# Splitting the value products of the prompt attention into fp32r halves, and moving the softmax weighing to GpSimd

## The chip, the cores and the metric

The kernel runs on one core of a Trainium2 chip. The metric is the device time of one execution in microseconds (us); lower is better. A core has five engines that run their own instruction lists and meet only through semaphores: TensorE (PE, matrix products and transposes, results in PSUM), VectorE (DVE), ScalarE (ACT), GpSimd (POOL) and SyncE (SP, here only DMA issue). PSUM has 8 banks of 128 partitions by 512 fp32 numbers; in this kernel `psA` to `psD` are two banks each, and `bank[0]` to `bank[7]` counts through them.

## The reference

One step of a one-layer decoder trunk in fp32, for a prompt of 1024 tokens and for 8 x 4 sampled tokens that share the weights. The input projection feeds a convolution group, a pooling group and an attention group ("NSA") of 8 query heads in 2 key/value groups of 4 heads, head size 64. The attention of the prompt has three branches, each with its own keys and values:

```python
s = jnp.einsum('bqgrd,bngd->bgrqn', q, kc).astype(jnp.float32) * scale + tbl[:, :, t5_bucket(dist)]
p_cmp = masked_softmax(s, dist >= 0)                       # compressed blocks, 63 keys
o_cmp = jnp.einsum('bgrqn,bngd->bqgrd', p_cmp.astype(vc.dtype), vc)
...                                                        # selected blocks: all earlier keys here
p = masked_softmax(s, (dist >= 0)[:, :, None])
o_slc = jnp.einsum('bgrqm,bgqmd->bqgrd', p.astype(vg.dtype), vg)
...                                                        # window of 512 keys
p = masked_softmax(s, mask)
o_win = jnp.einsum('bgrqk,bkgd->bqgrd', p.astype(vw.dtype), vw)
return gates[:, :, 0] * o_cmp + gates[:, :, 1] * o_slc + gates[:, :, 2] * o_win
```

Behind it come the output projection, RMSNorm, a gated feed-forward network of width 2816 and a last RMSNorm. With 1024 tokens there are 16 blocks of 64 keys, and the top-k takes 16, so the selected branch attends to every earlier key.

## The kernel before

The program is written out by hand for each engine; nothing is scheduled by a tool. It goes through stages: transposes and the input projection (to about 245 us), the sampled tokens (to about 345 us), the attention of the prompt (345 to 617 us), the output projection (to about 725 us), the feed-forward network and the last norm. The change is in the prompt attention and at its edges.

The prompt has 8 query tiles of 128 tokens (`i` = 0 to 7). For each, `ORDER` lists five groups: (g=0, br=1), (g=0, br=2), compressed, (g=1, br=1), (g=1, br=2). Branch 1 sees `128*(i+1)` keys, branch 2 at most 640. The compressed group serves both g at once. The four others are "dense": 32 dense groups, called by their number q in `DENSE`. `steps()` makes four steps for each q, one for each head r. In a step PE computes the scores of head (q, r) and then works off "tiles" of the group three places earlier (`LAG = 3`): a tile is 128 keys of all four heads, and the tiles of a group are spread over its four steps. There are 132 dense tiles and 8 compressed ones.

What happens to one head: PE writes the scores into PSUM (`p_score`, L1017 and L1018, two fp32r products), DVE adds the bias and finds the maximum (`p_biased_max`, L1814 to L1820), ACT takes the exponential into SBUF (`p_exp`, L1415, one step later), DVE computes 1/sum times the gate for a whole group (`group_weights`, L1858 and L1861) and multiplies each head by it (`weigh_head`, L1867). What happens to one tile: PE transposes 128 x 128 of each of the four heads into one turn bank (`turn`, L731), ACT copies the bank to one of three SBUF buffers `probT` (`drain`, L1312), and PE multiplies it with 128 columns of `kvtok`, two tiles later in its list (`p_values`, L1037 in plain fp32; L1028 for the compressed tile). The values of g=0 stand in columns 0 to 63 and those of g=1 in columns 64 to 127, with zeros beside them, so that one bank (6) collects both groups. `turn_bank` gives the tiles banks 4, 5 and 7 in turn, `turn_free` says which earlier tile must have been drained. When a query tile is complete ACT copies bank 6 to `featT` (`out_tile`, L1421) and PE may start the next.

fp32r is a format in which a product takes one pass over the array and loses low bits. Elsewhere in this kernel exactness is kept by splitting a number into a high part, which is its fp32r rounding, and a low part, the rest.

GpSimd's only work ahead of this stage is at L2127 to L2151: it places the values in `kvtok` (four instructions), splits keys and queries into high and low parts, and is then idle until the scores are done. SP waits for the split keys before it distributes them (`load_keys`, L649). At the end of the stage DVE makes the low parts of the first two output weight tiles (`rest_w`, L1884) and then those of the features (L1909), for which `fH` (L1457) comes from ACT.

## Time and profile before

| | |
|---|---|
| median of 3 runs | 1512.11 us (1511.27 to 1513.88) |
| profiled execution | 1512.36 us |
| its span, first to last instruction | 1510.2 us |
| busy: PE, DVE, ACT, POOL | 1451.0, 759.1, 477.7, 219.2 us |
| granted TensorE clock, mean | 0.987 |

The profiled execution is 2.2 us longer than its span, which is what lies around the program. "Busy" counts the time in which at least one instruction of the engine is recorded; neighbouring instructions of one engine overlap a little in the records, so the distance between two starts is the better measure of what one costs. A matrix product in plain fp32 is recorded as two instructions. Clock 1.00 is the granted TensorE clock at its upper level, 0.50 at the lower.

### The profile page before, as it was taken

How to read it: one execution, taken by the hardware profiler on the slowest of the kernel's cores; microseconds unless marked ns; L12 is line 12 of the kernel's file. 1: busy time of each engine (PE TensorE's matmuls, PEld its weight loads, DVE VectorE, ACT ScalarE, POOL GpSimd, SP SyncE). 2: the span in 40 equal slices, each digit the busy share in tenths (PEclk: the TensorE clock that was granted, in tenths of full speed). 3: DMA queues.
4: the chain of work that ended last, by engine and by line, in shares of the span. 5: the costliest groups of instructions: out<-in, count | busy, mean ns of one | idle time of the engine just before them, and what ended most of it. 6: DMA issues, size and time to landing. Idle time of an engine off the chain costs nothing.

```text
span 1510.2 us, 22117 instructions
## 1 busy us (share of the span) xinstructions
PE 1451.0 (96%) x8743; PEld 1330.9 (88%) x8743; DVE 759.1 (50%) x1535; ACT 477.7 (32%) x961; POOL 219.2 (15%) x251
## 2 busy tenths in 40 slices
PE   6999999888999999899999999999999999999996
PEld 6999988656666666699999999999999999999996
DVE  5499933226887776322424443524253344435257
ACT  5122124236776666422311211211121112111123
POOL 2114102520000000044220101010100101010105
PEclk9999999999999999999999999999999999999998
DMA  8731114943111102232110211202020202112012
GB/s 204 192 78 30 45 31 125 303 112 77 43 28 29 29 1 43 55 87 74 54 46 22 63 39 50 63 26 73 11 74 19 70 22 64 42 46 67 18 49 115
DMA packets 165815, 98.98 MB, mean 66 GB/s; under 512 B 35650, under 2 KB 160537, under 8 KB 165633
## 3 DMA queue, kind: packets, MB, share of 16 engines
q1 hardware_dynamic: 163217, 88.71, 21.5%
q0 software_dynamic: 2496, 8.88, 2.2%
q8 instruction: 69, 1.13, 0.3%
q14 instruction: 33, 0.27, 0.1%
HBM read 78.33 MB, written 13.19 MB: 61 GB/s over the span
## 4 chain that ended last, share of the span: by engine, by line
PE 82%; DVE 7%; SPq 3%; DMA 3%; ACT 2%; issue 2%; POOL 0%; POOLq 0%; DVEq 0%; ACTq 0%
PE psA L1065 16%; PE psB L1065 16%; PE psC L1065 16%; PE psD L1037 6%; PE psC L731 4%; DVE ybuf L1653 4%; DMA zraw<-in_w_in 2%; PE psD L731 2%; PE psA L782 2%; PE psA L1094 2%; PE psB L1094 2%; PE psC L1094 2%; PE psB L782 2%; PE psC L782 2%; PE psB L1017 1%
## 5 line engine op out<-in xcount | busy, mean ns | idle before, releaser
L1429 ACT CAST wH<-wraw 128x1024 fp32r<-128x1024 f32 (+1 forms) x132 | 86.7, 658 | 262.2 <-PE psC L1065 176.4
L2174 POOL TENSOR_TENSOR hid<-hid,rstdB 128x352 f32<-128x352 f32 x66 | 74.8, 1162 | 629.1 <-ACT hid L1490 629.1
L1037 PE MATMUL psD<-probTb,kvtok 128*128 128x512 f32 x264 | 135.7, 597 | 2.2 <-ACT featT L1421 2.1
L1884 DVE TENSOR_TENSOR wL<-wraw,wH 128x1024 fp32r<-128x1024 f32 (+1 forms) x132 | 107.2, 813 | 44.7 <-ACT wH L1429 44.7
L1065 PE MATMUL psA<-gH,wH 128*128 128x352 f32 x352 | 113.7, 323 | 0.0
L1065 PE MATMUL psB<-gH,wH 128*128 128x352 f32 x352 | 113.7, 323 | 0.0
L1065 PE MATMUL psC<-gH,wH 128*128 128x352 f32 x352 | 113.5, 322 | 0.0
L1065 PE MATMUL psA<-gH,wL 128*128 128x352 f32 x352 | 113.2, 322 | 0.0
L1065 PE MATMUL psB<-gH,wL 128*128 128x352 f32 x352 | 113.1, 321 | 0.0
L1065 PE MATMUL psA<-gL,wH 128*128 128x352 f32 x352 | 113.1, 321 | 0.0
L1065 PE MATMUL psB<-gL,wH 128*128 128x352 f32 x352 | 112.9, 321 | 0.0
L1065 PE MATMUL psC<-gL,wH 128*128 128x352 f32 x352 | 112.8, 321 | 0.0
L1065 PE MATMUL psC<-gH,wL 128*128 128x352 f32 x352 | 112.8, 320 | 0.0
L1653 DVE SCALAR_TENSOR_TENSOR ybuf<-glu,convw,ybuf 128x1296 f32<-128x1296 f32 x60 | 103.3, 1766 | 0.7
L1939 DVE TENSOR_TENSOR hid<-psA,rstdB 128x352 f32<-128x352 f32 x44 | 21.0, 520 | 160.7 <-PE psB L1065 160.6
L1947 DVE TENSOR_TENSOR hid<-psB,hid 128x352 f32<-128x352 f32 x22 | 11.5, 525 | 167.4 <-PE psC L1065 167.4
L1490 ACT ACTIVATE hid<-hid 128x352 f32<-128x352 f32 x66 | 29.9, 499 | 204.9 <-DVE hid L1939 204.9
L1312 ACT COPY probTb<-psC 128x512 f32<-128x512 f32 (+2 forms) x104 | 58.8, 565 | 46.7 <-PE psC L731 46.4
L1494 ACT CAST aH<-hid 128x352 fp32r<-128x352 f32 x66 | 31.5, 487 | 122.8 <-DVE hid L1947 121.8
L1065 PEld LDWEIGHTS psA<-gL,wH 128*128 128x128 f32 x352 | 66.4, 189 | 0.0
L1065 PEld LDWEIGHTS psB<-gH,wL 128*128 128x128 f32 x352 | 66.2, 188 | 0.0
L1065 PEld LDWEIGHTS psA<-gH,wH 128*128 128x128 f32 x352 | 66.0, 188 | 0.2
(426 smaller groups left out, 3898.7 us busy)
## 6 DMA issues: line engine op xcount, KB each, us to landing
wraw<-in_w_gu SPq DMA_DIRECT2D x44, 512.0 KB
wraw<-in_w_down SPq DMA_DIRECT2D x80, 128.0 KB
zraw<-in_w_in SPq DMA_DIRECT2D x12, 512.0 KB
xa<-in_x_prompt SPq DMA_DIRECT2D x8, 512.0 KB, 8.4
pages<-in_cache_cmp_kv SPq DMA_DIRECT2D x32, 128.0 KB, 2.4
qS<-qH SPq DMA_DIRECT2D x32, 128.0 KB, 2.4
qS<-qL SPq DMA_DIRECT2D x32, 128.0 KB, 2.4
xs<-in_x_prompt SPq DMA_DIRECT2D x8, 512.0 KB, 3.8
```

Source lines behind the costliest of these rows:

```text
L731: return pe.transpose(dst, src, ident[0:n, 0:n])
L782: mm = pe.matmul(bank[3 * (m % 2) + n][:, 0:w], wt[:, m % 2, k, :], mv[:, k, c0:c0 + w], start=(k == 0 and wt is zH and mv is xH), stop=(k ...
L1037: mm = pe.matmul(o, kvtok[:, kt, vc:vc + P], pt, start=first, stop=((g, br) == ORDER[-1] and x == len(g_tiles(n)) - 1))
L1065: mm = pe.matmul(bank[3 * par + n][:, 0:cw], wt[:, par, k, :], mv[:, k, at:at + cw], start=(k == 0 and mv is mH and wt is wH), stop=(k == ...
L1094: mm = pe.matmul(b[:, 0:cw], wt[:, par, k, :], mv[:, k, c0:c0 + cw], start=False, stop=(k == KD - 1 and wt is wL))
L1312: op = sc_.copy(dst, srcfn(bank[turn_bank(u)]))
L1429: sc_.copy(wH[:, par, 0:nk, :], wraw[:, par, 0:nk, :]).then_inc(s["wH_done"], 1)
L1490: sc_.activation(hid[:, n, :], hid[:, n, :], ACT.Silu).then_inc(s["silu_done"], 1)
L1494: sc_.copy(aH[:, par, x // 2, at:at + cw], hid[:, n, :]).then_inc(s["aH_done"], 1)
L1653: op = dve.scalar_tensor_tensor(out=y, in0=x, scalar=w, in1=y, op0=ALU.mult, op1=ALU.add)
L1884: dve.tensor_tensor(wL[:, par, 0:nk, :], wraw[:, par, 0:nk, :], wH[:, par, 0:nk, :].bitcast(F32), ALU.subtract).then_inc(s["wL_done"], 1)
L2174: pool.tensor_tensor(hid[:, n, :], hid[:, n, :], rstdB[:, c0:c0 + cw], ALU.mult).then_inc(s["up_scaled"], 1)
```

## The change

Values: GpSimd writes each value block as 64 high and 64 low columns into `vS` (which lies over `kvtok`) with 64 small instructions that wait for one another. Each group g now has an accumulator bank of its own, 6 and 7. The tile is kept as `probH`, ACT's fp32r rounding of the turn bank, and `probL`, which a new DVE instruction per tile (`rest_tile`) computes as bank minus `probH`. A value product becomes two fp32r products of 128 x 512. The result stands in two halves of the bank (with high values and with low values), which ACT (`out_half`) and DVE (`out_sum`) add into `featT`, for each (i, g).

The compressed product becomes two fp32 products, on rows 0 to 63 and 64 to 127, into the two banks. The turn banks are 4 and 5 only; a dense turn bank is free when `rest_tile` has read it. The weighing of 112 of 128 heads goes to GpSimd, which does them group after group; head 3 of the 16 dense groups of query tiles 0 to 3 stays on DVE.

```diff
@@ -245,7 +251,7 @@
 
     if U_C <= u < U_C + 2 * NB:
         return 4 + (u - U_C) % 4
-    return 4 + u % 2 if u < U_T else (4, 5, 7)[(u - U_T) % 3]
+    return 4 + u % 2
 
 
 def turn_free(u):
...
@@ -254,10 +260,13 @@
         return u - 4 if u >= U_C + 4 else U_C - 1
     if U_C + 2 * NB <= u < U_C + 2 * NB + 2:
         return U_C + 2 * NB - 1
-    return u - 2 if u < U_T else U_T - 1 if u < U_T + 3 else u - 3
-
-
-OUT_AFTER = {i: max(u for k, u in PUNIT.items() if k[0] == "t" and GROUPS[k[1]][0] == i) for i in range(NT)}
+    return u - 2
+
+
+OUT_AFTER = {(i, g): max(u for k, u in PUNIT.items() if k[0] == "t" and GROUPS[k[1]][:2] == (i, g))
+             for i in range(NT) for g in range(KVH)}
+BY_DVE = [(n, GQ - 1) for n in DG if GROUPS[n][0] < 4]
+DENSE_T = {k: m for m, k in enumerate([k for k in PUNIT if k[0] == "t" and k[1] in DENSE])}
 
 
 LASTQ = [(n, m) for n in range(3) for m in range(KD)]
...
@@ -369,6 +378,9 @@
         vcT = at("vcT", [P, KC_N - 1], 166144)
         vctok = at("vctok", [P, 3, P], 167424)
         probT = [probTb[:, k, :] for k in range(NPT)]
+        probH = at("probH", [P, NPT, 512], 158720, F32R)
+        probL = [at(f"probL{k}", [P, 512], o, F32R) for k, o in enumerate((54528, 164864, M_S + 2528))]
+        vS = at("vS", [P, NT + 1, KVG], M_Z, F32R)
         cmpw = at("cmpw", [P, 3, 8, P], 168960)
         cmph = at("cmph", [P, 2, KC_N], 158720)
         cmps = at("cmps", [P, 2, KC_N], 161312)
...
@@ -472,7 +484,9 @@
 
         def wait_drained(eng, key):
 
-            if key in DRAINED_D:
+            if key in DENSE_T:
+                eng.wait_ge(s["pl_done"], DENSE_T[key] + 1)
+            elif key in DRAINED_D:
                 eng.wait_ge(s["turn_drain_d"], DRAINED_D[key])
             else:
                 eng.wait_ge(s["turn_drain"], DRAINED_A[key])
...
@@ -1021,21 +1035,25 @@
             def p_values(n, x):
 
                 i, g, br = GROUPS[n]
-                pt = probT[PUNIT[("t", n, x)] % NPT]
+                slot = PUNIT[("t", n, x)] % NPT
                 wait_drained(pe, ("t", n, x))
-                o = bank[6]
                 if br == 0:
-                    mm = pe.matmul(o, vcBD, pt, start=False, stop=False)
+                    if i:
+                        pe.wait_ge(s["o_ev"], 2 * i)
+                    pt = probT[slot]
+                    pe.matmul(bank[6], vcBD[0:HD, :], pt[0:HD, :], start=False, stop=False)
+                    mm = pe.matmul(bank[7], vcBD[HD:P, :], pt[HD:P, :], start=True, stop=False)
                 else:
                     first = x == 0 and (g, br) == ORDER[0]
                     if first and i == 0:
-                        pe.wait_ge(s["v_pad"], 4)
+                        pe.wait_ge(s["v_pad"], 4 * 2 * NT)
                     elif first:
-                        pe.wait_ge(s["o_ev"], i)
+                        pe.wait_ge(s["o_ev"], 2 * i - 1)
                     kt = x if br == 1 else i + 1 - g_width(n) // P + x
                     vc = 256 * br + P * g
-                    mm = pe.matmul(o, kvtok[:, kt, vc:vc + P], pt, start=first,
-                                   stop=((g, br) == ORDER[-1] and x == len(g_tiles(n)) - 1))
+                    last = br == 2 and x == len(g_tiles(n)) - 1
+                    pe.matmul(bank[6 + g], vS[:, kt, vc:vc + P], probH[:, slot, :], start=first, stop=False)
+                    mm = pe.matmul(bank[6 + g], vS[:, kt, vc:vc + P], probL[slot][:, :], start=False, stop=last)
                 mm.then_inc(s["probT_used"], 1)
 
             for _, _, jobs, tiles in steps():
...
@@ -1044,7 +1062,8 @@
                 for n, x in tiles:
                     if n in DENSE:
                         if x == 0:
-                            pe.wait_ge(s["scaled"], GQ * (DENSE[n] + 1))
+                            pe.wait_ge(s["scaled"], weighed(DENSE[n])[0])
+                            pe.wait_ge(s["scaled_d"], weighed(DENSE[n])[1])
                         turn(("t", n, x), [(P * r, P, prob(n, r)[:, P * x:P * x + P]) for r in range(GQ)])
                     else:
                         pe.wait_ge(s["cmp_scaled"], GROUPS[n][0] + 1)
...
@@ -1415,11 +1434,12 @@
                 sc_.activation(prob(n, r)[:, 0:w], p_scores(n, r)[:, 0:w], ACT.Exp,
                                bias=nmax[:, job % 4:job % 4 + 1], scale=-1.0, accum_out=psums[q % 4][:, r:r + 1]).then_inc(s["exp_done"], 1)
 
-            def out_tile(i):
-
-                sc_.wait_ge(s["probT_used"], OUT_AFTER[i] + 1)
-                sc_.copy(featT[:, 4:8, P * i:P * i + P], bank[6].rearrange("p (r t) -> p r t", r=GQ)
-                         ).then_inc(s["o_ev"], 1)
+            def out_half(i, g):
+
+                sc_.wait_ge(s["probT_used"], OUT_AFTER[i, g] + 1)
+                gp, other = slice(HD * g, HD * g + HD), slice(HD * (1 - g), HD * (1 - g) + HD)
+                sc_.copy(featT[gp, 4:8, P * i:P * i + P], bank[6 + g][other, :].rearrange("p (r t) -> p r t", r=GQ)
+                         ).then_inc(s["o_half"], 1)
 
             def round_w(w, par, nk):
...
@@ -1854,7 +1874,8 @@
                 rc = precs[q % 4]
                 dve.wait_ge(s["exp_done"], NSJ + LASTJOB[n] + 1)
                 if q >= 4:
-                    dve.wait_ge(s["scaled"], GQ * (q - 3))
+                    dve.wait_ge(s["scaled"], weighed(q - 4)[0])
+                    dve.wait_ge(s["scaled_d"], weighed(q - 4)[1])
                 dve.reciprocal(rc, psums[q % 4]).then_inc(s["sum_read"], 1)
                 dve.wait_ge(s["sum_read"], q + 1)
                 c = KVC + NH * br + GQ * g
@@ -1864,14 +1885,22 @@
             def weigh_head(n, r):
 
                 p = prob(n, r)[:, 0:g_width(n)]
-                dve.tensor_scalar(p, p, precs[DENSE[n] % 4][:, r:r + 1], None, ALU.mult).then_inc(s["scaled"], 1)
-
-            def turn_copy(key):
-
-                pu = PUNIT[key]
-                dve.wait_ge(s["turn_fill"], UNIT[key] + 1)
-                dve.wait_ge(s["probT_used"], pu - NPT + 1)
-                dve.tensor_copy(probT[pu % NPT], bank[4 + UNIT[key] % 2]).then_inc(s["turn_drain_d"], 1)
+                dve.tensor_scalar(p, p, precs[DENSE[n] % 4][:, r:r + 1], None, ALU.mult).then_inc(s["scaled_d"], 1)
+
+            def rest_tile(n, x):
+
+                key = ("t", n, x)
+                slot = PUNIT[key] % NPT
+                dve.wait_ge(s["turn_drain"], DRAINED_A[key])
+                dve.tensor_tensor(probL[slot][:, :], bank[turn_bank(UNIT[key])], probH[:, slot, :].bitcast(F32), ALU.subtract
+                                  ).then_inc(s["pl_done"], 1)
+
+            def out_sum(i, g):
+
+                gp = slice(HD * g, HD * g + HD)
+                o = featT[gp, 4:8, P * i:P * i + P]
+                dve.wait_ge(s["o_half"], 2 * i + g + 1)
+                dve.tensor_tensor(o, bank[6 + g][gp, :].rearrange("p (r t) -> p r t", r=GQ), o, ALU.add).then_inc(s["o_ev"], 1)
 
             def link2(op):
                 chain[0] += 1
@@ -1894,12 +1923,17 @@
                 if 0 <= old < len(DG):
                     if head == 0:
                         group_weights(DG[old])
-                    weigh_head(DG[old], head)
+                    if (DG[old], head) in BY_DVE:
+                        weigh_head(DG[old], head)
                 if r == 3 and rider(q) is not None:
                     c_scale(rider(q))
                 for n, x in tiles:
-                    if ("t", n, x) in DRAINED_D:
-                        turn_copy(("t", n, x))
+                    if n in DENSE:
+                        rest_tile(n, x)
+                    for o, last in OUT_AFTER.items():
+                        if last == PUNIT["t", n, x] - 4:
+                            out_sum(*o)
+            out_sum(NT - 1, 1)
             for w in range(2):
                 rest_w(w, w, KD)
...
@@ -2122,13 +2156,6 @@
 
             pool.wait_ge(s["qbd_done"], 1)
             pool.wait_ge(s["stores"], 16 * STORES)
-            for br in (1, 2):
-                c = 256 * br
-                pool.tensor_copy(kvtok[:, 0:NT, c:c + HD], kvtok[:, 0:NT, c + P:c + P + HD]).then_inc(s["v_pad"], 1)
-            for br in (1, 2):
-                c = 256 * br
-                pool.wait_ge(s["v_pad"], br)
-                pool.memset(kvtok[:, 0:NT, c + HD:c + HD + P], 0.0).then_inc(s["v_pad"], 1)
             pool.wait_ge(s["cmpw_used"], 4)
             pool.memset(pcmp, 0.0).then_inc(s["prob_zero"], 1)
...
@@ -2138,6 +2165,23 @@
                 count[0] += 1
                 op.then_inc(s["pool"], 1)
                 pool.wait_ge(s["pool"], count[0])
+
+            pads = [0]
+
+            def pad(op):
+
+                pads[0] += 1
+                op.then_inc(s["v_pad"], 1)
+                pool.wait_ge(s["v_pad"], pads[0])
+
+            for i in range(NT):
+                for br in (1, 2):
+                    c = 256 * br
+                    for g in range(KVH):
+                        v = kvtok[:, i, c + P + HD * g:c + P + HD * g + HD]
+                        vh = vS[:, i, c + P * g:c + P * g + HD]
+                        pad(pool.tensor_copy(vh, v))
+                        pad(pool.tensor_tensor(vS[:, i, c + P * g + HD:c + P * g + P], v, vh.bitcast(F32), ALU.subtract))
 
             old = slice(0, T)
             in_turn(pool.tensor_copy(keysH[:, :, :], keysT[:, :, old]))
...
@@ -2149,9 +2193,16 @@
                 cols = slice(P * i, P * i + P)
                 pool.tensor_tensor(qL[:, :, cols], qT[:, :, cols], qH[:, :, cols].bitcast(F32), ALU.subtract
                                    ).then_inc(s["split_done"], 1)
+            for q, n in enumerate(DG):
+                pool.wait_ge(s["rec_done"], q + 1)
+                for r in range(GQ):
+                    if (n, r) in BY_DVE:
+                        continue
+                    p = prob(n, r)[:, 0:g_width(n)]
+                    pool.tensor_scalar(p, p, precs[q % 4][:, r:r + 1], None, ALU.mult).then_inc(s["scaled"], 1)
             pool.wait_ge(s["score_mm"], NSJ + NJ)
             pool.memset(xs[0][:, NT, :], 0.0).then_inc(s["x_pad"], 1)
-            pool.wait_ge(s["o_ev"], NT)
+            pool.wait_ge(s["o_ev"], 2 * NT)
```

Three places show how the instructions stand in each engine's list. First VectorE, in the steps behind the compressed weighing of query tile 5 (`psA`, `psB` are score banks, `ISA` is the bias and minimum in one instruction, `narrow` and `wide` hold exponentials). Before:

```order
TENSOR_TENSOR narrow<-narrow,small_115 128x8x47
TENSOR_REDUCE small_115<-psA 128x1
ISA psA,nmax<-psA,btab,small_115 128x256
ISA nmax 128x1
TENSOR_SCALAR wide<-wide,small_115 128x768
TENSOR_REDUCE small_115<-psB 128x1
ISA psB,nmax<-psB,btab,small_115 128x256
ISA nmax 128x1
RECIPROCAL small_115<-small_115 128x4
TENSOR_TENSOR small_115<-small_115,kvtok 128x4
TENSOR_SCALAR narrow<-narrow,small_115 128x640
```

Now, at the same place:

```order
TENSOR_TENSOR narrow<-narrow,small_120 128x8x47
TENSOR_TENSOR probL_105<-psC,probH 128x512
TENSOR_REDUCE small_120<-psA 128x1
ISA psA,nmax<-psA,btab,small_120 128x256
ISA nmax 128x1
TENSOR_TENSOR probL_106<-psC,probH 128x512
TENSOR_TENSOR probL_107<-psC,probH 128x512
TENSOR_REDUCE small_120<-psB 128x1
ISA psB,nmax<-psB,btab,small_120 128x256
ISA nmax 128x1
RECIPROCAL small_120<-small_120 128x4
```

The weighing (`TENSOR_SCALAR`) is gone from the list, and one subtraction from a turn bank stands there for each tile of the step.

Second TensorE, in the last query tile. `cpk` is the identity, so rows with it are the transposes of a tile; `kS` marks scores. Before:

```order
MATMUL psC<-cpk,narrow 128x128 x4
MATMUL psD<-probTb,kvtok 128x512
MATMUL psC<-cpk,narrow 128x128 x4
MATMUL psD<-probTb,kvtok 128x512
MATMUL psB<-kS,qS_111 128x512
```

Now:

```order
MATMUL psC<-cpk,narrow 128x128 x4
MATMUL psD<-probH,vS 128x512
MATMUL psD<-probL_107,vS 128x512
MATMUL psC<-cpk,narrow 128x128 x4
MATMUL psD<-probH,vS 128x512
MATMUL psD<-probL_105,vS 128x512
MATMUL psB<-kS,qS_116 128x512
```

One product per tile has become two, and the place of the scores between them is the same.

Third VectorE at the end of the stage, where `wL` are the output weights' low parts and `fL` those of the features. Before:

```order
TENSOR_SCALAR wide<-wide,small_115 128x1024 x2
RECIPROCAL small_115<-small_115 128x4
TENSOR_TENSOR small_115<-small_115,kvtok 128x4
TENSOR_SCALAR narrow<-narrow,small_115 128x640 x4
TENSOR_TENSOR wL<-wraw,wH 128x1024 x2
TENSOR_TENSOR fL<-featT,fH 128x1056 x8
```

Now:

```order
TENSOR_TENSOR probL_105<-psC,probH 128x512
TENSOR_TENSOR probL_106<-psC,probH 128x512
TENSOR_TENSOR probL_107<-psC,probH 128x512
TENSOR_TENSOR featT<-psD,featT 64x4x128
TENSOR_TENSOR wL<-wraw,wH 128x1024 x2
TENSOR_TENSOR fL<-featT,fH 128x1056 x8
```

The two `wL` instructions now stand behind the last tile's work and the last sum of halves.

## Rows read from the trace of the kernel before

**Rows 1.** Busy time by stretches of the stage (us from:to, length, engines, clock).

```profile
345.00:371.50 26.50, 23.03 (x125) 18.20 (x123) 21.17 (x122) 18.79 (x73) 0.00 (x0) 0.87 0.24 61
371.50:581.20 209.70, 202.97 (x1005) 141.14 (x1005) 167.57 (x496) 144.58 (x309) 0.00 (x0) 1.00 0.11 26
581.20:617.00 35.80, 35.68 (x166) 21.38 (x163) 11.70 (x26) 19.75 (x37) 0.21 (x1) 1.00 0.23 45
```

**Rows 2.** The same view of L1867 alone, VectorE's weighing.

```profile
371.50:581.20 209.70, 49.49 (x94) 1.00 0.11 26
```

**Rows 3.** TensorE in order of time (start, length): fp32r scores, transposes, value product.

```profile
567.55 0.40 PE L1017 MATMUL psA<-kS,qS 128*128 128x512 f32 x1
...
568.02 0.60 PE L731 MATMUL psC<-cpk,narrow 128*128 128x128 f32 x4
568.46 1.02 PE L1037 MATMUL psD<-probTb,kvtok 128*128 128x512 f32 x2
569.32 0.60 PE L731 MATMUL psC<-cpk,narrow 128*128 128x128 f32 x4
```

**Rows 4.** VectorE in order of time in the first stage: a bank minus its rounding.

```profile
25.16 1.27 DVE L1614 TENSOR_TENSOR xL<-psD,xH 128x512 fp32r<-128x512 f32 x2
26.36 1.26 DVE L1605 SCALAR_TENSOR_TENSOR xn<-xa,small,gB 128x1024 f32<-128x1024 f32 x1
```

**Rows 5.** VectorE in order of time: finding the least, and weighing.

```profile
541.20 0.56 DVE L1818 TENSOR_REDUCE small<-psA 128x1 f32<-128x384 f32 x1
541.80 0.49 DVE L1820 CUSTOM_DVE_ANT_0 psA<-psA,btab,small 128x256 f32<-128x256 f32 x1
...
549.75 0.55 DVE L1867 TENSOR_SCALAR narrow<-narrow,small 128x640 f32<-128x640 f32 x1
550.22 0.95 DVE L1818 TENSOR_REDUCE small<-psB 128x1 f32<-128x768 f32 x1
```

**Rows 6.** Order of time behind the last scores: casts, a turn, its drain.

```profile
597.68 2.00 ACT L1429 CAST wH<-wraw 128x1024 fp32r<-128x1024 f32 x2
...
601.70 0.60 PE L731 MATMUL psC<-cpk,wide 128*128 128x128 f32 x4
...
602.39 0.58 ACT L1312 COPY probTb<-psC 128x512 f32<-128x512 f32 x1 [0.71 <-PE psC L731]
```

**Rows 7.** Order of time at the end of the stage.

```profile
616.39 0.49 PE L1088 MATMUL psA<-cpk,xs 128*128 128x128 f32 x3
...
616.59 0.59 ACT L1421 COPY featT<-psD 128x512 f32<-128x512 f32 x1 [1.94 <-PE psD L1037]
...
618.18 2.43 DVE L1909 TENSOR_TENSOR fL<-featT,fH 128x1056 fp32r<-128x1056 f32 x2 [17.05 <-ACT fH L1457]
...
619.49 0.44 PE L1094 MATMUL psA<-fH,wH 128*128 128x384 f32 x1 [2.62 <-DVE fL L1909]
```

**Rows 8.** GpSimd in order of time ahead of the stage.

```profile
249.78 4.27 POOL L2109 TENSOR_SCALAR qbd<-qT 64x16 f32<-64x16 f32 x16
...
290.03 1.89 POOL L2143 CAST keysH<-keysT 128x2048 fp32r<-128x2048 f32 x1
```

**Rows 9.** SyncE in order of time: the first keys handed out.

```profile
321.65 2.45 SPq L649 DMA_DIRECT2D kS<-keysH  x4
```

**Rows 10.** L2174, a GpSimd product: count, durations min/median/max, first and last start.

```profile
L2174 POOL TENSOR_TENSOR hid<-hid,rstdB x66: 943/950/1976, 741.8 to 1430.0; 128x352 f32<-128x352 f32 x66
```

**Rows 11.** Order of time: VectorE and GpSimd at once, output projection.

```profile
629.62 0.83 POOL L2162 TENSOR_TENSOR accA<-featT 128x384 f32<-128x384 f32 x1 [12.18 <-ACT featT L1471]
629.64 0.62 DVE L1918 SCALAR_TENSOR_TENSOR gL<-psA,gain,gH 128x384 fp32r<-128x384 f32 x1 [2.01 <-ACT featT L1471]
```

**Rows 12.** Busy time by stretches, where the clock fell.

```profile
348.00:351.50 3.50, 1.95 (x13) 1.42 (x11) 3.17 (x21) 1.18 (x6) 0.00 (x0) 0.97 0.39 96
351.50:354.50 3.00, 2.59 (x12) 2.55 (x12) 2.58 (x20) 2.56 (x12) 0.00 (x0) 0.50 0.26 65
```

**Rows 13.** TensorE in order of time: products over 64 rows, two row halves by turns.

```profile
270.62 8.95 PE L914 MATMUL psA<-ckT,cmpw 64*128 64x322 f32 x64 [0.98 <-DVE cvT L1735]
```

25 lines of the change are left out of this document (14 added, 11 removed).

## The prediction

> **What bounds the kernel now.** I began with the page's busy times: TensorE 1451.0 of 1510.2 us, so what matters is where that changes. The change touches the prompt attention, 345 to 617 us. The view of busy time by stretches, cut at the moments when query tiles 0 and 6 are copied out, shows three parts [rows 1]. In the long middle part (209.7 us, query tiles 1 to 6) TensorE is busy for 203.0 us and VectorE for 167.6, ScalarE for 144.6, GpSimd not at all. In the last part (35.8 us, the values of tile 7 and, after its first groups, no more scores) TensorE is all but full and VectorE has 11.7 us of work. So TensorE sets the pace, but in the middle VectorE follows at 80%. Next I read the order of time for what one instruction costs by the distance of starts, and last the end of the stage, where the first output product waits for VectorE's `fL` [rows 7].
>
> **TensorE: less work.** A plain fp32 value product holds the engine from 568.46 to 569.32, 0.86 us; an fp32r product of 512 columns takes half of 567.55 to 568.02, 0.235 us [rows 3]. Two of them are 0.47, so each dense tile gives back 0.39 us, 132 tiles 51.5 us. The compressed product becomes two over 64 rows each. The compression shows that form: 64 instructions, 32 products of 322 columns, in 8.95 us, 0.28 each [rows 13], where 0.86 x 322/512 = 0.54 would be due. The two row halves run side by side, and a pair of 512 columns costs 2 x 0.28 x 512/322 = 0.89 us, the same as today's 0.86: nothing, at most 8 x 0.86 = 7 us if different banks kept them apart. If TensorE alone set the pace, the stage would be shorter by 51.5.
>
> **VectorE: more work.** `rest_tile` has the form of an instruction in the first stage, bank minus rounding, 128 x 512 into fp32r: two of them hold the engine from 25.16 to 26.36, 0.60 us each [rows 4]. In the middle part there are 102 tiles (8 + 12 + 16 + 20 + 22 + 24): +61.2. `out_sum` is as long over 64 partitions, 12 x 0.60 = +7.2. What goes is weighing: 94 instructions, 49.5 us there [rows 2]; about 12 of them stay (head 3 of tiles 1 to 3, narrow ones, an estimate of 0.38 us each, 4.6 us), and each removed one frees 0.08 us less than its length, since the next starts at 550.22 when it began at 549.75 and took 0.55 [rows 5]. So 44.9 - 82 x 0.08 = 38.3 go. VectorE: 167.6 - 38.3 + 61.2 + 7.2 = 197.7 us, against 203.0 - 102 x 0.39 = 163.2 on TensorE. The bound changes hands. ScalarE keeps its copies and gets a second output copy per query tile (12 x 0.59 instead of 6), 148 us: no bound.
>
> How full can VectorE be? In one head's chain each step waits 0.04 us for the one before (541.20 + 0.56 to 541.80 [rows 5]), about 4 us over 96 heads: 201.7. Then the new loop: a turn bank is free only when TensorE filled it, ScalarE copied it and VectorE subtracted. From a turn's start to its copy's start is 0.69, the copy 0.58 [rows 6], the subtraction with its tail 0.67, two handovers of 0.06: 2.06 us for two banks, 1.03 per tile. In a step with scores VectorE spends 1.3 to 1.4 us on the head and 0.60 on each of one or two tiles, 1.9 to 2.6 us, and a turn that starts when the earlier subtraction ends is copied 1.3 us later, while VectorE works on the head. The loop is thus mostly covered; I allow 5.5 us of stalls (24 groups, some 0.2 us each at the step where a group begins, and the narrow tiles 1 and 2, where steps are short). Middle part: 207.2 instead of 209.7, **-2.5 us**. Bounds: 201.7 without a stall (-8.0); VectorE full to 90%, 197.7/0.90 = 219.7 (+10.0).
>
> First part: 4 tiles and 2 sums on VectorE (+3.6) against some 20 narrow weighings less; **-0.5**, bounds -3 and +3. GpSimd's work: 112 heads, 62,500 columns. No row has its multiplication by a column at this size. The nearest one-input row is the cast, 1.89 us for 2048 columns, 0.92 ns each; the slowest two-input row has a median of 0.95 us for 352 columns, 2.7 ns [rows 8, 10]. That is 1.1 or 2.9 us per head of 1024 with 0.15 us for the start. The group must be ready 1.75 groups after its factors, 17 us for tile 7, and four such heads are 4.4 or 11.6 us: covered at either end. I take the first.
>
> Last part: while the last scores run (4 steps, 8 tiles), VectorE needs 4 x (1.34 + 2 x 0.60) + 0.4 = 10.6 us. Behind them are 18 dense tiles and a compressed one with nothing between, where the bank loop rules: 18 x 1.03 + 1.2 = 19.7. ScalarE's two weight casts of 2.00 us [rows 6] stand in the middle of that and nothing hides them any longer. Sum 32.3 instead of 35.8, **-3.5 us** (bounds -5.5, if the casts find a gap, and 0).
>
> End: from the last product to the first output product are 616.39 to 619.49, 3.10 us [rows 7]. Now: copy until 617.18, sum of halves until 617.85, then both `wL`, which used to run at 599.91 with 1.22 us each [rows 6] and now stand behind the last sum, until 620.2, then `fL`, 1.25: 621.5. **+2.0 us**; the seven further `fL` set the pace afterwards as they do now, so it isn't won back.
>
> Head of the stage: 64 small GpSimd instructions ahead of the keys' split. The multiplication of 16 columns takes 0.267 (4.27/16) [rows 8]; with 64 columns and a wait behind each 0.3 to 0.4 us, 19 to 26 us in all. The keys were split at 296.5 and handed out at 321.65 [rows 9], 25 us later, so this is covered to within 1 us: 0, at worst +5.
>
> Sum: -2.5 - 0.5 - 3.5 + 2.0 = **-4.5 us**. The profiled execution took 1512.36 (span 1510.2 and 2.2 around it), 0.25 above the median of the runs: 1507.9 us.
>
> **Does GpSimd hold VectorE up?** Both used at once is in the rows: a VectorE instruction with one input in PSUM and one in SBUF, started 0.02 us behind a GpSimd product, took 0.62 us [rows 11], its usual time. `rest_tile` has that form. But L2174 on GpSimd, next to VectorE instructions with two SBUF inputs, took 0.943 us at least and 1.976 at most [rows 10]: something is waited for. The Trainium skill (SBUF — State Buffer, "SBUF: two separate sides") has the rule: the two engines share one pair of ports as an exclusive lock, held for a whole instruction, against VectorE instructions in a two-port mode or with two SBUF inputs. By that rule the rest of each tile passes freely, in agreement with the 0.62, while the kept weighings and the small products with two SBUF inputs can be made to wait.
>
> **The rivals.**
> 1. *The bank loop isn't covered (slower).* Place: steps in which VectorE reaches `rest_tile` before ScalarE's copy, because the exponential of the head before stands ahead of it on ScalarE. Price: at 90% fullness the middle is +10.0 instead of -2.5, in all +8.0: 1520.4. It turns slower when fullness falls below 197.7/(209.7 + 2 + 3) = 92%. For it: today's 80% and the short steps of the first tiles; against it: today VectorE waits for a TensorE that now has 44 us to spare.
> 2. *No stall at all.* -8.0 - 2 - 5 + 2.0 = -13: 1499.4. For it: three buffers and the copy's 1.3 us inside the head's time.
> 3. *The lock.* 32 factor products, 16 kept weighings, 16 compressed ones have two SBUF inputs or two ports: 64 instructions, each waiting at most for one GpSimd instruction of 0.7 to 2 us, half of that on average when GpSimd is busy, 30 to 60% of the time: 64 x 0.35 x 0.3 = 7 to 64 x 1.0 x 0.6 = 38 us on the bound engine, with my first value +7 - 4.5: 1515, at the far end 1546. Against it: the factors are made just before GpSimd gets the group.
> 4. *The clock.* The clock went to its lower level (0.50, 1.2 GHz) at 351.5, behind 3.5 us in which TensorE was busy for 1.95 [rows 12]. It will now be less busy in tiles 1 and 2. One more such spell of 6 us costs some 3 us: 1511.
> 5. *TensorE still sets the pace*, -51.5: 1461. VectorE's 197.7 us speak against it, unless a subtraction were far cheaper than in rows 4.
>
> **Chances.** Forecast (fullness 94 to 98%) 0.48, about 1503 to 1512; rival 1 0.22; rival 2 0.16; rival 3 0.07; rival 4 and late keys 0.05; rival 5 0.02. This kernel's measurement tells 0.2%, 3 us, from no change: faster is below 1509.1, slower above 1515.1. Two thirds of the forecast, and rivals 2 and 5, are faster: 0.51. The rest of the forecast with parts of 1, 3 and 4: same 0.22. Slower 0.27. Range: 1499 to 1522, which leaves out rival 5, the far ends of 1 and 3 and little else.
>
> **What would show it.** The profile after should have TensorE at about 0.79 of the middle part and VectorE at 0.95 or more; `rest_tile` at 0.67 us and 0.60 from start to start; value products as pairs of 0.235 us; the tiles behind the last scores 1.03 us apart; about 5.1 us between the last value product and the first output product; GpSimd's weighing at about 1 ns a column. I am wrong if VectorE has idle time of more than 15 us in the middle, and then the releaser of that idle time says whether it was ScalarE's copy (rival 1) or a length above 0.67 (rival 3).

## The result, and the profile after

The change made the kernel slower, by about 1%.

| | before | after |
|---|---|---|
| median | 1512.84 us (1511.27 to 1513.88, 4 runs) | 1529.72 us (1525.66 to 1531.33, 4 runs) |
| ratio, 95% interval | | 1.0108 [1.0084, 1.0133] |
| profiled execution, span | 1512.36, 1510.2 | 1531.33, 1529.5 |
| busy: PE, DVE, ACT, POOL | 1451.0, 759.1, 477.7, 219.2 | 1425.1, 802.1, 481.4, 418.3 |

The forecast was 1507.9 us with a range of 1499 to 1522; the time lies 8 us above the upper end. TensorE has 26 us less to do and VectorE 43 more, as forecast. To see where the time went, the stage is cut at the same moments as in [rows 1]: first score, copy of each finished query tile out of the accumulator, first output product. Lengths are in us, taken from the starts in the order of time of each run (PE and ACT):

| run | tile 0 | 1 | 2 | 3 | 4 | 5 | 6 | 7 | end |
|---|---|---|---|---|---|---|---|---|---|
| before | 26.0 | 20.2 | 26.0 | 33.9 | 39.7 | 43.2 | 46.7 | 35.9 | 2.90 |
| after | 26.1 | 23.8 | 28.2 | 35.2 | 40.2 | 42.5 | 45.0 | 48.9 | 4.92 |

The 19.3 us by which the span grew are: 1.5 in which the stage starts later (first score at 346.37 instead of 344.84), 0.0 in tile 0, +4.9 in the middle part, tiles 1 to 6 (forecast -2.5), +13.0 in the last query tile (forecast -3.5), +2.0 at the end (forecast +2.0), and -2.2 behind the first output product. Two thirds are in one place.

Busy time by stretches of after (as [rows 1]: length, PE, PEld, DVE, ACT, POOL, clock, DMA share, GB/s): the middle part, then the last query tile in three pieces.

```profile
373.00:587.75 214.75, 180.00 (x1017) 139.28 (x1018) 198.80 (x530) 146.48 (x315) 153.05 (x85) 0.98 0.10 25
587.75:602.70 14.95, 13.11 (x81) 9.83 (x80) 11.69 (x28) 9.66 (x19) 13.57 (x6) 1.00 0.00 1
602.70:620.66 17.96, 2.46 (x14) 1.39 (x12) 1.51 (x4) 3.91 (x6) 5.92 (x5) 0.67 0.42 89
620.66:636.70 16.04, 14.98 (x70) 10.51 (x70) 8.76 (x14) 7.37 (x14) 0.00 (x0) 0.83 0.00 1
```

The third row holds the loss: 18 us in which PE is busy for 2.46, DVE for 1.51 and ACT for 3.91. Only DMA works (0.42, 89 GB/s). Rows of the order of time around that stretch in after, grouped by engine: PE's last product before the wait, GpSimd's last two groups and the clearing, SyncE, ScalarE, VectorE, and PE's first work behind the wait:

```profile
604.85 0.40 PE L1056 MATMUL psD<-probL,vS 128*128 128x512 f32 x1
...
589.72 11.31 POOL L2202 TENSOR_SCALAR wide<-wide,small 128x1024 f32<-128x1024 f32 x4 [1.38 <-DVE small L1882]
601.00 7.47 POOL L2202 TENSOR_SCALAR narrow<-narrow,small 128x640 f32<-128x640 f32 x4
608.41 0.21 POOL L2204 MEMSET xs<- 128x128 f32 x1
...
608.69 0.37 SPq L687 DMA_DIRECT2D xs<-in_x_prompt  x1
...
610.19 1.01 SPq L699 DMA_DIRECT2D wraw<-in_w_out  x1
...
616.27 1.04 ACT L1449 CAST wH<-wraw 128x1024 fp32r<-128x1024 f32 x1 [12.94 <-DMA wraw<-in_w_out]
618.35 1.04 ACT L1449 CAST wH<-wraw 128x1024 fp32r<-128x1024 f32 x1 [1.04 <-DMA wraw<-in_w_out]
619.30 1.07 ACT L1331 CAST probH<-psC 128x512 fp32r<-128x512 f32 x2
...
619.92 1.29 DVE L1895 TENSOR_TENSOR probL<-psC,probH 128x512 fp32r<-128x512 f32 x2 [15.85 <-ACT probH L1331]
...
620.66 1.12 PE L745 MATMUL psC<-cpk,wide 128*128 128x128 f32 x4 [15.42 <-DVE probL L1895]
```

It is read from the bottom up. PE waits 15.42 us for VectorE's `probL`; VectorE 15.85 us for ScalarE's `probH`; ScalarE, which works in order, stands 12.94 us at the cast of an output weight whose bytes have not come; SyncE issued that load at 610.19, behind the input block `xs`, at 608.69; and `load_xs(0)` waits for one small clearing on GpSimd, `MEMSET xs`, which ran at 608.41, behind the last of the 112 weighings. In before, SyncE and GpSimd did this 21 us earlier, as their order of time there shows:

```profile
587.65 0.21 POOL L2153 MEMSET xs<- 128x128 f32 x1 [246.18 <-PE psB L1018]
...
589.43 0.58 SPq L685 DMA_DIRECT2D wraw<-in_w_out  x1
```

The cast then came at 597.68 and waited for nothing [rows 6]. The engine named by PE's wait (VectorE) had no fault in it; it took four steps back to reach GpSimd.

GpSimd's rate was mis-estimated too. Groups of after by shape (count, busy us, mean ns, idle before):

```profile
L2202 POOL TENSOR_SCALAR narrow<-narrow,small 128x640 f32<-128x640 f32 x32 | 59.8, 1888 | 16.6 <-DVE small L1882 16.6
L2202 POOL TENSOR_SCALAR wide<-wide,small 128x1024 f32<-128x1024 f32 x8 | 22.6, 2848 | 5.1 <-DVE small L1882 5.1
...
L2202 POOL TENSOR_SCALAR narrow<-narrow,small 128x256 f32<-128x256 f32 x6 | 5.4, 924 | 5.0 <-DVE small L1882 5.0
...
L2202 POOL TENSOR_SCALAR wide<-wide,small 128x128 f32<-128x128 f32 x6 | 3.6, 614 | 9.3 <-DVE small L1882 9.3
```

From 256 to 1024 columns it goes from 924 to 2848 ns, 2.5 ns a column with 0.3 us around it, where I took 0.92 ns from the cast [rows 8] and kept 2.7 as the far end.

What the subtraction costs (count, shortest/median/longest in ns), and then who waits around it: two rows each of the waits of DVE and of PE between 373 and 586 us of after (us in total, times, longest):

```profile
L1895 DVE TENSOR_TENSOR probL<-psC,probH x132: 672/689/694, 355.1 to 634.6; 128x512 fp32r<-128x512 f32 x132
```

```profile
DVE probL L1895 <- ACT probH L1331: 3.4, 12, 0.7
DVE small L1838 <- PE psA L1032: 1.4, 2, 0.8
```

```profile
PE psC L745 <- DVE probL L1895: 14.8, 17, 2.4
PE psB L1031 <- ACT narrow L1434: 4.2, 4, 1.8
```

VectorE is busy for 198.8 of 214.75 us (92.6%); PE, with 35 us to spare, waits above all for VectorE to give a turn bank back.

### The profile page after: what moved, and what is told of

It reads as the page before. It is cut to its first block, busy times and chain, and to the rows that moved or that the text cites. A ratio compares the mean times of both kernels' runs of the same rounds, so it can differ in the third digit from the quotient of the medians.

```text
span 1529.5 us, 22397 instructions
## 1 busy us (share of the span) xinstructions
PE 1425.1 (93%) x8759; PEld 1332.5 (87%) x8759; DVE 802.1 (52%) x1571; ACT 481.4 (31%) x969; POOL 418.3 (27%) x423
## 4 chain that ended last, share of the span: by engine, by line
PE 76%; DVE 12%; issue 4%; ACT 3%; POOL 2%; DMA 1%; SPq 1%; POOLq 0%; DVEq 0%; ACTq 0%
PE psA L1084 16%; PE psB L1084 16%; PE psC L1084 16%; PE psA L796 4%; PE psB L796 4%; PE psC L796 4%; PE psC L745 3%; DVE small L1838 3%; DVE probL L1895 2%; PE psA L1113 2%; PE psC L1113 2%; PE psB L1113 2%; PE psD L745 1%; DVE ybuf L1673 1%; DVE psB L1840 1%
## 5 line engine op out<-in xcount | busy, mean ns | idle before, releaser
L2202 POOL TENSOR_SCALAR wide<-wide,small 128x640 f32<-128x640 f32 (+7 forms) x56 | 100.9, 1820 | 43.2 <-DVE small L1882 43.2
L1895 DVE TENSOR_TENSOR probL<-psC,probH 128x512 fp32r<-128x512 f32 x132 | 89.3, 688 | 32.8 <-ACT probH L1331 31.6
L2202 POOL TENSOR_SCALAR narrow<-narrow,small 128x640 f32<-128x640 f32 (+4 forms) x56 | 85.5, 1545 | 35.9 <-DVE small L1882 35.9
L1510 ACT ACTIVATE hid<-hid 128x352 f32<-128x352 f32 x66 | 29.9, 498 | 206.3 <-DVE hid L1973 206.3
L1331 ACT CAST probH<-psC 128x512 fp32r<-128x512 f32 x132 | 76.7, 584 | 37.8 <-PE psC L745 37.1
L745 PE MATMUL psC<-cpk,wide 128*128 128x128 f32 x320 | 51.3, 286 | 21.1 <-DVE probL L1895 21.0
```

Source lines behind the costliest of these rows:

```text
L745: return pe.transpose(dst, src, ident[0:n, 0:n])
L1331: op = sc_.copy(dst, srcfn(bank[turn_bank(u)]))
L1895: dve.tensor_tensor(probL[slot][:, :], bank[turn_bank(UNIT[key])], probH[:, slot, :].bitcast(F32), ALU.subtract).then_inc(s["pl_done"], 1)
L2202: pool.tensor_scalar(p, p, precs[q % 4][:, r:r + 1], None, ALU.mult).then_inc(s["scaled"], 1)
```

## The experiments

There are three sets: e1, e2, e4, e5; then e3, e6, e7, e8; then e10 to e13. Each set has its own runs of before (medians 1513.75, 1513.24 and 1511.64 us of 13, 21 and 8 runs), so the ratios are compared, not the medians. Here are the per-tile lengths that the verdicts rest on:

| run | start | 0 | 1 | 2 | 3 | 4 | 5 | 6 | 7 | end | span |
|---|---|---|---|---|---|---|---|---|---|---|---|
| before | 344.8 | 26.0 | 20.2 | 26.0 | 33.9 | 39.7 | 43.2 | 46.7 | 35.9 | 2.90 | 1510.2 |
| after | 346.4 | 26.1 | 23.8 | 28.2 | 35.2 | 40.2 | 42.5 | 45.0 | 48.9 | 4.92 | 1529.5 |
| e1_pad_early | 345.9 | 26.0 | 23.8 | 28.2 | 35.2 | 40.2 | 42.4 | 45.0 | 32.8 | 4.92 | 1511.8 |
| e2_weigh_dve | 346.0 | 28.0 | 25.2 | 31.9 | 38.8 | 46.3 | 49.5 | 52.2 | 43.6 | 4.92 | 1555.6 |
| e4_short_rest | 344.0 | 25.3 | 20.5 | 24.4 | 30.5 | 36.7 | 39.1 | 42.0 | 28.6 | 4.92 | 1483.7 |
| e5_hybrid | 344.4 | 25.6 | 22.0 | 26.7 | 34.1 | 38.9 | 41.4 | 44.6 | 30.8 | 4.92 | 1500.8 |
| e3_two_banks | 343.6 | 26.3 | 20.2 | 26.0 | 33.9 | 39.7 | 43.2 | 46.7 | 35.9 | 2.91 | 1509.5 |
| e7_before_pool | 346.2 | 25.2 | 18.1 | 25.1 | 33.5 | 39.7 | 43.2 | 46.8 | 50.9 | 2.90 | 1522.1 |
| e8_before_pool_pad | 346.0 | 25.2 | 18.1 | 25.1 | 33.5 | 39.7 | 43.2 | 46.8 | 35.9 | 2.91 | 1504.9 |
| e6_pad_wl | 343.7 | 26.1 | 23.7 | 28.2 | 35.3 | 40.2 | 42.5 | 45.0 | 33.1 | 3.02 | 1507.7 |
| e10_late_split | 343.7 | 25.7 | 19.2 | 24.7 | 33.8 | 38.9 | 41.4 | 44.6 | 30.8 | 4.92 | 1493.6 |
| e11_late_half | 342.5 | 26.9 | 19.1 | 24.7 | 35.7 | 39.3 | 41.6 | 44.6 | 32.7 | 4.92 | 1499.1 |
| e12_late_split_wl | 343.8 | 25.8 | 19.1 | 24.7 | 33.8 | 38.9 | 41.4 | 44.6 | 30.8 | 3.02 | 1492.8 |
| e13_late_half_wl | 344.6 | 25.8 | 19.1 | 24.7 | 35.4 | 39.3 | 41.6 | 44.6 | 32.1 | 3.02 | 1497.1 |

### The clearing, alone

After, with the clearing moved forward in GpSimd's list, ahead of the weighing of the 17th dense group. The cleared block lies over low parts of the queries of tiles 1 and 2, so it waits until those are handed out.

```diff
             for q, n in enumerate(DG):
                 pool.wait_ge(s["rec_done"], q + 1)
+                if q == 16:
+                    for k in range(3):
+                        pool.wait_ge(s[f"q_in{k}"], 128)
+                    pool.memset(xs[0][:, NT, :], 0.0).then_inc(s["x_pad"], 1)
...
-            pool.wait_ge(s["score_mm"], NSJ + NJ)
-            pool.memset(xs[0][:, NT, :], 0.0).then_inc(s["x_pad"], 1)
```

> The clearing of the last block of xs[0] stands behind GpSimd's 17th group instead of behind all 32; it waits for the query loads that still read its place. Theory 1: in the last part the weight loads started late (608.7 us) because SyncE waited for that clearing, ScalarE's weight cast waited 12.9 us for them, and with it every copy of a turn bank. Then the cast should find its data, the 15.9 us without VectorE work should go, and the time falls by 13 to 15 us to 1515 to 1517, ratio to the kernel before 1.001 to 1.003. Rival: the last part is long because of the bank loop and the fallen clock, and GpSimd's place is an accident; then the time falls by less than 4 us, to 1526 or more.

1512.64 us (1507.64 to 1516.36, 10 runs), ratio to before 0.9991 [0.9979, 1.0004], where after has 1.0108; between the two profiled executions the span falls by 17.7 us. The first load of the output stage goes out with the last score, as in before, and ScalarE casts both weights without a wait:

```profile
592.55 0.37 SPq L687 DMA_DIRECT2D xs<-in_x_prompt  x1
```

```profile
602.75 2.00 ACT L1449 CAST wH<-wraw 128x1024 fp32r<-128x1024 f32 x2
```

Tiles 0 to 6 are unchanged to 0.1 us, the last goes from 48.90 to 32.83. The median is 2 to 4 us below what I expected; in the spans 16.1 us of the 17.7 are the last tile, and the rest lies ahead of the stage and behind it. So the step that made the kernel slower is the place of that one instruction of 0.21 us; all else in the change comes out at no difference that can be measured.

The same from the other side: before, with only the weighing given to GpSimd (all 128 heads; value products, banks and subtractions as before), once with the clearing left behind it and once with it forward.

```diff
-                    weigh_head(DG[old], head)
+                    pass
...
+            for q, n in enumerate(DG):
+                pool.wait_ge(s["rec_done"], q + 1)
+                for r in range(GQ):
+                    p = prob(n, r)[:, 0:g_width(n)]
+                    pool.tensor_scalar(p, p, precs[q % 4][:, r:r + 1], None, ALU.mult).then_inc(s["scaled"], 1)
             pool.wait_ge(s["score_mm"], NSJ + NJ)
             pool.memset(xs[0][:, NT, :], 0.0).then_inc(s["x_pad"], 1)
```

That is e7; e8 has in addition the four lines of `if q == 16` shown above, and the two last lines here are gone.

> The kernel before with all 128 heads weighed on GpSimd and its clearing of xs[0] left behind them; plain fp32 products, three turn banks. Theory 1 says that GpSimd's queue alone makes the loads late: the last factors are made at about 589 us, four heads of 640 columns take 4 x 1.89 us, so the loads start at some 597 instead of 588 and ScalarE's cast at 598 waits until about 607: last part +6 to +9 us, the time 1517 to 1523. Rival (GpSimd's work has no such effect): 1506 to 1514.

> As e7, with the clearing behind the 17th group. The loads start when the scores are done. VectorE is relieved of some 57 us that were hidden under TensorE; TensorE at 203 of 209.8 us leaves 3 to 5 us to win: 1508 to 1513. If GpSimd's instructions hold up VectorE's (port lock), VectorE's 160 small instructions with two SBUF inputs would lengthen and it comes out above 1516.

e7: 1523.41 us (3 runs), ratio 1.0064 [1.0045, 1.0082]. e8: 1507.26 us (5 runs), ratio 0.9954 [0.9938, 0.9971]. Every tile is the same in both but the last, 50.9 against 35.9. In e7:

```profile
593.20 5.61 POOL L2156 TENSOR_SCALAR narrow<-narrow,small 128x640 f32<-128x640 f32 x3
598.75 0.21 POOL L2158 MEMSET xs<- 128x128 f32 x1
```

```profile
606.52 1.04 ACT L1429 CAST wH<-wraw 128x1024 fp32r<-128x1024 f32 x1 [11.72 <-DMA wraw<-in_w_out]
```

The late clearing thus costs 15 us with plain value products too, where I had expected 6 to 9: I had left out that GpSimd is still at the group before when the last factors are made, and that the clock falls in the wait (both are taken up below). And taking all weighing off VectorE, which was not the bound (its busy time in the middle falls from 168.2 to 130.8 us), wins 3.5 us in tiles 1 to 6 (206.3 instead of 209.8), 2.1 of them in tile 1.

### Which engine sets the pace of the middle

After, with all weighing back on VectorE. GpSimd then weighs nothing, but its loop still waits for each group's factors.

```diff
-BY_DVE = [(n, GQ - 1) for n in DG if GROUPS[n][0] < 4]
+BY_DVE = [(n, r) for n in DG for r in range(GQ)]
```

> All 128 heads weighed on VectorE again, everything else as changed; GpSimd is free, so its clearing is in time. Theory 2: VectorE bounds the middle. It gets 112 weighings back, some 40 us in the middle part and 4 in the first, and loses nothing but the 13 to 15 us of the late loads: 1529.7 - 14 + 40 = 1550 to 1560. Rival: the loop of two turn banks bounds the middle and VectorE has room beside it; then the weighings fall into that room and the time is 1515 to 1530.

And e1 with a subtraction of 64 columns instead of 512. It leaves the low part of the exponentials out of the value product; the second product takes the high part once more, so that TensorE's work stays.

```diff
-                dve.tensor_tensor(probL[slot][:, :], bank[turn_bank(UNIT[key])], probH[:, slot, :].bitcast(F32), ALU.subtract
+                dve.tensor_tensor(probL[slot][:, 0:64], bank[turn_bank(UNIT[key])][:, 0:64], probH[:, slot, 0:64].bitcast(F32), ALU.subtract
...
-                    mm = pe.matmul(bank[6 + g], vS[:, kt, vc:vc + P], probL[slot][:, :], start=False, stop=last)
+                    mm = pe.matmul(bank[6 + g], vS[:, kt, vc:vc + P], probH[:, slot, :], start=False, stop=last)
```

> With the early clearing. The subtraction of a tile covers 64 of 512 columns and the second value product reads the high half again, so the low part of the weights is left out; TensorE's work, the number of VectorE instructions and all waits stay. Theory 2: VectorE loses 102 x 0.45 = 46 us in the middle and 10 more elsewhere, TensorE becomes the bound at some 165 to 175 us instead of 214.8, the last part goes to TensorE's 0.9 us per tile: 1515 - 45 = 1465 to 1475. If instead ScalarE or the exponentials held the middle, it stays above 1495.

e2: 1557.62 us, 1.0287 [1.0266, 1.0307]. Its last tile (43.6) is long for the old reason as well, since the clearing stands behind the wait for the last group's factors even where nothing is weighed, and so only its middle part is used here. The clearing and what PE waits for in the last tile of e2:

```profile
634.16 0.50 POOL L2204 MEMSET xs<- 128x128 f32 x1 [291.54 <-DVE small L1882]
...
646.77 1.11 PE L745 MATMUL psC<-cpk,wide 128*128 128x128 f32 x4 [8.18 <-DVE probL L1895]
```

e4: 1486.31 us, 0.9816 [0.9796, 0.9835]. Middle parts of e1, e2 and e4, columns as above:

```profile
372.00:586.70 214.70, 179.33 (x1014) 138.84 (x1014) 198.85 (x529) 146.26 (x315) 153.10 (x87) 0.98 0.10 25
```

```profile
374.00:617.90 243.90, 188.49 (x1015) 143.71 (x1014) 233.09 (x613) 147.56 (x315) 0.00 (x0) 0.95 0.09 23
```

```profile
369.40:562.40 193.00, 171.68 (x1014) 137.05 (x1015) 157.77 (x529) 145.79 (x314) 153.70 (x87) 1.00 0.12 28
```

34.2 us more on VectorE make the middle 29.2 longer; 41.1 us less make it 21.7 shorter. The first of these says that VectorE sets the pace in after: work that is no part of the bank loop comes through at 85%. The second alone would not, since a shorter subtraction also gives the turn bank back sooner. Nor did e4 reach the 1465 to 1475 us that I expected: even with a cheap subtraction the middle takes 193, with TensorE, now the longer of the two, busy for 171.7 (89%). The fuller engine is busy for 95.6% of the middle in e2, where it is VectorE by 45 us, for 92.6% in e1, where it leads by 20, and for 89% in e4, where 14 us lie between them.

### The two turn banks

Before with two banks in place of three:

```diff
-    return 4 + u % 2 if u < U_T else (4, 5, 7)[(u - U_T) % 3]
+    return 4 + u % 2
...
-    return u - 2 if u < U_T else U_T - 1 if u < U_T + 3 else u - 3
+    return u - 2
```

> The kernel before with turn banks 4 and 5 instead of 4, 5 and 7, nothing else. There a bank is free after ScalarE's copy, 0.69 + 0.58 + 0.06 = 1.33 us after the start of its transposes, two banks 0.67 us per tile, under TensorE's 1.30. If two banks as such cost the middle part its fullness, it shows here: +3 to +8 us, most of it in tiles 1 and 2. Theory 2 (a bank held until VectorE has subtracted, and VectorE full) expects no change: within 2 us of 1513.8.

1513.07 us (10 runs), 0.9995 [0.9984, 1.0007]; no tile behind the first differs by more than 0.1 us (tile 0 by 0.3). While a plain fp32 product of 0.86 us stands between the turns, the third bank was worth nothing. Whether a third bank would help the split tiles no run shows: bank 7 is taken there.

### Fewer split tiles

e1 with two of three dense tiles split; every third keeps a plain fp32 product with the high and low columns of `vS` (which gives the same two halves).

```diff
-DENSE_T = {k: m for m, k in enumerate([k for k in PUNIT if k[0] == "t" and k[1] in DENSE])}
+DENSE_T = {k: m for m, k in enumerate([k for k in PUNIT if k[0] == "t" and k[1] in DENSE and PUNIT[k] % 3 < 2])}
...
+                    if ("t", n, x) in DENSE_T:
...
+                    else:
+                        mm = pe.matmul(bank[6 + g], vS[:, kt, vc:vc + P].bitcast(F32), probT[slot], start=first, stop=last)
```

> With the early clearing. Two of three dense tiles are split as changed, the third is multiplied in plain fp32 (0.86 us on TensorE, nothing on VectorE, its turn bank is free after ScalarE's copy). Middle part: VectorE 198.8 - 34 x 0.60 = 178, TensorE 163 + 34 x 0.39 = 176. Theory 2 (two busy engines, the longer sets the pace, filled to 92%): 178/0.92 = 194 instead of 214.8, the time 1515 - 21 = 1490 to 1498. Rival (the bank loop sets the pace): two thirds of the tiles keep the loop, the gain is a few us: 1508 to 1514.

1505.69 us (4 runs), 0.9948 [0.9931, 0.9964]: better than the rival's 1508 to 1514, but far from the 1490 to 1498 of my theory. The middle takes 207.6, where 194 was expected: VectorE is busy for 182.4 us of it and TensorE for 185.4, so that neither leads. And, which I had not expected, the last tile takes 30.8 instead of 32.8: a plain tile needs no `rest_tile`, so its bank comes back after the copy.

In e8, e5 and e1 the first tiles are best without a split and the later ones with it. The next kernel puts the two together: the split only from query tile 3 on, and all heads weighed on GpSimd.

```diff
-BY_DVE = [(n, GQ - 1) for n in DG if GROUPS[n][0] < 4]
+BY_DVE = []
...
+DENSE_T = {... if k[0] == "t" and k[1] in DENSE and GROUPS[k[1]][0] >= 3 and PUNIT[k] % 3 < 2])}
```

> After with the clearing early, GpSimd weighs all heads, and only two of three dense tiles of query tiles 3 to 7 are split, the rest of the tiles keep plain fp32 products on (high and low) value columns. Theory: splitting pays only where TensorE has many tiles per head and costs where steps are short (query tiles 1 and 2 took 23.8 and 28.2 us split, 18.1 and 25.1 plain with GpSimd's weighing). Then query tiles 0 to 2 take 25.2, 18.1, 25.1 as in e8_before_pool_pad, 3 to 7 take 34.1, 38.9, 41.4, 44.6, 30.8 as in e5_hybrid, in all 258.2 plus 4.9 at the end: 7.9 us less than e8 and 5.8 less than e5, about 1499.5. Rival: the loss of query tiles 1 and 2 comes from the two sums of halves and the two accumulators, not from the split; then they take 20 to 22 and 26 to 27 and the whole is 1502 to 1505.

1496.12 us (1495.42 to 1500.34, 4 runs), with about 1499.5 expected; ratio 0.9904 [0.9879, 0.9929]: twice the gain of e8 and e5, and after stands at 1.0108. Tiles 1 and 2 take 19.2 and 24.7, so their loss in after came from the split (and the eight weighings VectorE kept there), not from the second accumulator or the sums; 1.1 us of tile 1 stay unaccounted for against e8. From the first score to the first output product e10 takes 263.9 us, e8 270.3 and before 274.7. So 4.3 us of the gain come with the weighing alone, as in e8, and 6.4 with the split: -4.5 in tiles 3 to 6, -5.1 in the last, +1.2 in tiles 0 to 2 and +2.0 at the end. Busy time of e10 in tiles 2, 3 and 6:

```profile
388.50:413.20 24.70, 24.70 (x116) 16.25 (x116) 18.59 (x64) 19.54 (x49) 21.16 (x16) 1.00 0.18 44
413.20:447.00 33.80, 29.01 (x170) 22.38 (x169) 29.58 (x82) 23.35 (x51) 28.02 (x19) 1.00 0.13 32
...
527.20:571.90 44.70, 41.48 (x225) 30.45 (x224) 38.09 (x91) 31.46 (x62) 36.96 (x17) 1.00 0.01 1
```

Unsplit, TensorE is full (24.70 of 24.70). In the first split tile both engines have about 29 us of work in 33.8, and nothing is won against e8's 33.5; in tile 6 the split wins 2.1 us. e11 splits every second tile of 3 to 6 instead, and all of 7:

```diff
+... and GROUPS[k[1]][0] >= 3 and (PUNIT[k] % 2 or GROUPS[k[1]][0] == 7)])}
```

> As e10_late_split, but every second tile of query tiles 3 to 6 is split, and all of 7. Theory (VectorE sets the pace where tiles are split): VectorE gets 15 subtractions less in the middle, 9 us, TensorE 15 x 0.39 = 6 us more, 191 us of products against 173 us; then query tiles 3 to 6 are 2 to 4 us shorter than e10's if VectorE was the bound there, and as long or up to 2 us longer if the two engines were even. The last query tile takes 32.8 as in e1_pad_early instead of 30.8. About 1498 to 1503.

1501.57 us (5 runs), 0.9937 [0.9916, 0.9958]. Tile 3 is 1.9 us longer than e10's and tile 4 0.4, none is shorter: giving VectorE less and TensorE more did not help, which speaks against VectorE as the bound at two thirds. It is not shown, for the rule changes a second thing: the turn banks alternate from tile to tile, so with every second tile split all split tiles of a stretch use the same bank. No run parts the two.

### The low parts of the output weights

e1 with both `wL` computed in eight pieces of 256 columns, one behind each of eight of the last subtractions, instead of behind the last sum (e6); the same on e10 (e12); and the same with the rule shown last (e13).

```diff
+                    piece = TAIL.get((n, x))
+                    if piece is not None:
+                        w, k0 = divmod(2 * piece, KD)
+                        dve.wait_ge(s["wH_done"], w + 1)
+                        op = dve.tensor_tensor(wL[:, w, k0:k0 + 2, :], wraw[:, w, k0:k0 + 2, :],
+                                               wH[:, w, k0:k0 + 2, :].bitcast(F32), ALU.subtract)
...
-            for w in range(2):
-                rest_w(w, w, KD)
```

```diff
+... and GROUPS[k[1]][0] >= 3 and (PUNIT[k] % 2 or GROUPS[k[1]][0] == 7 and PUNIT[k] % 3 < 2)])}
```

> e1 and the first two weight remainders on VectorE cut into eight pieces of 256 columns that stand behind single tiles of the last two groups, instead of behind the last sum. The time from the last copy of the attention to the first output product should go from 4.92 to 2.9 us or below, as in the kernel before; each piece takes 0.33 us of VectorE, which waits about 0.4 us in each of these tiles. Expected 2 us less than e1: 1510 to 1512. If the pieces lengthen the bank loop by their own time, the last part grows by 2 us and nothing is won.

> As e10_late_split, with the low parts of the two output weights computed in eight pieces between the last subtractions. Theory: the bank loop leaves VectorE gaps there, so the last query tile takes the same (to +0.5) and the end takes 3.0 us instead of 4.9, as in e6_pad_wl: 1.5 to 2 us less than e10, about 1497.7. Rival: with plain tiles between the split ones the loop is no longer the bound and the pieces are in the way: 0 to 1 us won.

> As e12_late_split_wl, but every second tile of query tiles 3 to 6 is split and two of three in 7. By the two theories of e11_late_half and e12_late_split_wl: query tiles 3 to 6 as e11's, query tile 7 and the end as e12's, 1496 to 1501; it tells whether half or two thirds is the better share when the last query tile is alike.

e6: 1513.11 us (10 runs), 1.0000 [0.9988, 1.0013], not told from e1 and above the 1510 to 1512 that I expected. e12: 1495.47 us (1493.84 to 1499.48, 4 runs), 0.9897 [0.9871, 0.9924]. e13: 1498.22, 0.9906 [0.9881, 0.9931]. The traces agree with the theory, the times are too coarse for it: the end goes from 4.92 to 3.02 us in all three, the last tile gets 0.0 (e12) or 0.3 us (e6) longer. Order of time of VectorE in e12, two subtractions and their pieces in the last tile:

```profile
593.29 0.69 DVE L1899 TENSOR_TENSOR probL<-psC,probH 128x512 fp32r<-128x512 f32 x1 [0.50 <-ACT probH L1335]
593.89 0.41 DVE L1944 TENSOR_TENSOR wL<-wraw,wH 128x256 fp32r<-128x256 f32 x1
594.23 0.68 DVE L1899 TENSOR_TENSOR probL<-psC,probH 128x512 fp32r<-128x512 f32 x1
594.83 0.75 DVE L1944 TENSOR_TENSOR wL<-wraw,wH 128x256 fp32r<-128x256 f32 x2
596.39 0.69 DVE L1899 TENSOR_TENSOR probL<-psC,probH 128x512 fp32r<-128x512 f32 x1 [0.81 <-ACT probH L1335]
```

e12 has the lowest median of the kernels that compute all of it, 1.0% below before and 2.1% below after by the ratios. Its interval overlaps e10's and e13's: that these forms gain 1% is shown, which of the three is best is not.

## Why the prediction was wrong

**The step that failed: what stands behind the weighing on GpSimd.** The prediction asked of the 112 weighings whether TensorE gets its groups in time ("covered at either end"), and that was right: in after the profile puts no wait of PE's products down to GpSimd, and 0.2 us of its weight loads'. It did not ask what GpSimd's list holds behind them: the clearing, for which `load_xs(0)`, the weight loads, ScalarE's casts and then the whole bank loop wait. The price is 16.1 us (48.90 to 32.83, after against e1) and 15.0 without the split (e7 against e8). Of the rivals none had it. It could have been read from the diff, where the loop stands two lines above `x_pad`. So the term that failed is the last part: -3.5 forecast, +13.0 measured. The delay of the clearing has two parts in after. The last score ends at 593.02 and the last exponential at 596.72; VectorE, with subtractions ahead of them in its list, has the last factors ready at 600.51; GpSimd is at the group before until 601.0 (8.0 us behind the last score) and then weighs four heads (7.4 us). All but 0.5 us of the first part is there at any rate of GpSimd: in e2, where it weighs nothing, the clearing starts 9.0 us behind the last score. At the 2.7 ns a column that I kept as the far end, four heads of 640 columns are 6.9 us.

**GpSimd's rate, mis-sized.** 0.92 ns a column taken, 2.5 and 0.3 us measured; 186 us in all instead of some 75. For the groups' handover it cost nothing; in the clearing's delay of after it is the second part, where the copy's rate would have given 3.0 us. In e7 it weighs more: the last factors are ready at 588.2, but GpSimd is at the group before until 591.3 and clears at 598.75.

**Middle part, -2.5 forecast, +4.9 measured: stalls, as in rival 1.** The sums were right: VectorE 197.7 forecast and 198.8 measured, a subtraction 0.69 us long and 0.60 from start to start, the ten kept weighings in it 4.3 us (4.6 for twelve). The mis-sized term is the stalls. I allowed 4 us of handovers and 5.5 of waits; VectorE is idle for 214.75 - 198.80 = 15.95 us, of which the waits that the profile lists are 8.4 (for ScalarE's `probH` 3.4, for scores 5.0) and the small ones 7.6. That is the sign which the prediction named, more than 15 us; but only the 3.4 us are the wait that rival 1 describes. That the waits for scores come of the same loop, since PE itself waits 14.8 us for turn banks there, is my reading and not shown. Fullness 92.6%, between the forecast's 95.4 and rival 1's 90%, and close to the 92% at which I put the turn to slower: e1, which has this and the end's +2.0 but not the late clearing, is at no difference. (The chances of a faster time add up to 0.50, not 0.51.) The condition held as well: the loss is in the narrow tiles 1 and 2, +5.7 us together, while 5 and 6 win 2.5. And e10, with two of three tiles split and none in tiles 1 and 2, takes 202.5.

**First part, -0.5.** 0.0 in tile 0. The stage starts 1.5 us later, ahead of GpSimd's first weighing; the start of the stage lies between 342.5 and 346.4 in the fourteen traces and is no later in e5, e6, e10 to e13 than in before, though they have the 64 small instructions too. Those took 22.5 us (291.86 to 314.36, forecast 19 to 26), and the keys were out in time.

**Last part, -3.5.** With the clearing out of the way e1 takes 32.83, forecast 32.3. The copies of the bank loop show the period:

```profile
627.54 0.59 ACT L1331 CAST probH<-psC 128x512 fp32r<-128x512 f32 x1 [0.32 <-PE psC L745]
...
629.71 0.59 ACT L1331 CAST probH<-psC 128x512 fp32r<-128x512 f32 x1 [0.38 <-PE psC L745]
```

In after, 2.17 us for two tiles here and 2.10 for the next two, 1.03 each forecast. So the period of the loop is within 6% of the one that the prediction had. In e4, with the short subtraction, this tile takes 28.6 us.

**End, +2.0.** 2.90 to 4.92, the length of both `wL`:

```profile
637.41 2.36 DVE L1913 TENSOR_TENSOR wL<-wraw,wH 128x1024 fp32r<-128x1024 f32 x2
```

e6 and e12 take it back to 3.02 by moving them, which confirms the cause.

**TensorE.** Two fp32r products instead of one plain one: PE's busy time in the middle falls from 203.0 to 180.0, by 23.0 where 39.8 were forecast. The price of a tile was forecast rightly: where PE does not wait it takes 0.90 us (transposes at 550.68 and again at 551.58 in after) instead of 1.30 [rows 3], 0.40 less. The sum of busy time depends on more: the same 1014 instructions are busy for 171.7 us in e4, 179.3 in e1 and 188.5 in e2, the more PE waits between them (a product behind a pause records 0.48 to 0.50 us, and in a row one starts 0.24 behind the other) and the lower its clock (1.00, 0.98, 0.95). e4's 171.7 is the nearest to the forecast's 163.2. The compressed pair ran side by side (553.02 and 553.03, below), as forecast from [rows 13]. But with its second halves it holds PE until the next score at 554.08, 1.06 us, where 0.89 were forecast and 0.86 were spent before.

```profile
553.02 0.69 PE L1044 MATMUL psD<-probTb,vctok 64*128 64x512 f32 x1
553.03 0.69 PE L1045 MATMUL psD<-probTb,vctok 64*128 64x512 f32 x1
```

**The lock, rival 3.** As a cost it is rejected, but it left traces. The 32 factor products of the dense groups on VectorE take 161 to 165 ns in after and in before. Of the eight larger ones, for the compressed groups, four took 0.85 us more in sum than the 168 ns of before, and three kept weighings 0.24 us more: 1.1 us, where the rival has 7 to 38. The longest, with the next VectorE instruction and with the GpSimd work at that time, two instructions in one row, of which the second starts at 447.66:

```profile
447.86 0.62 DVE L1866 TENSOR_TENSOR small<-small,kvtok 128x8 f32<-128x8 f32 x1
448.51 0.48 DVE L1867 TENSOR_TENSOR narrow<-narrow,small 128x312 f32<-128x312 f32 x1
...
445.80 3.75 POOL L2202 TENSOR_SCALAR wide<-wide,small 128x640 f32<-128x640 f32 x2
```

In e2, where GpSimd weighs nothing, all eight took 167 or 168 ns. The Trainium skill (SBUF — State Buffer, "SBUF: two separate sides") names as locked out only VectorE instructions in a two-port mode or with two SBUF inputs, which leaves the subtraction free, and so far the runs agree: it is at most 694 ns beside a GpSimd that is busy for 71% of the middle. That the other engine is fully blocked for the whole instruction, as the same section says, they do not show: both VectorE instructions above have two SBUF inputs and ended while the GpSimd instruction ran on to 449.55, and the second took its usual 0.48 us.

**The clock, rival 4.** The granted clock fell to 0.73 in 416 to 420, behind 4 us in which PE was busy for 2.70, and to 0.50 from 610 to 626, behind the long wait:

```profile
412.00:416.00 4.00, 2.70 (x16) 1.84 (x14) 3.83 (x14) 2.03 (x5) 3.60 (x3) 1.00 0.46 114
416.00:420.00 4.00, 2.89 (x11) 2.21 (x12) 3.86 (x13) 2.51 (x6) 1.12 (x1) 0.73 0.01 2
...
624.00:626.00 2.00, 2.00 (x8) 1.56 (x7) 1.38 (x3) 0.75 (x2) 0.00 (x0) 0.50 0.03 8
626.00:628.00 2.00, 1.92 (x14) 1.35 (x12) 1.29 (x2) 1.05 (x2) 0.00 (x0) 0.99 0.00 0
```

e10 has 1.00 in all of tiles 1 to 6. The drop follows PE's waits and comes on top of them. Behind the long wait the traces price it. Counted from the start of the last tile, PE's first work behind the wait starts 14.2 us later in after than in e1, and the last value product 16.1 later: 1.9 us are lost while the clock stands at 0.50. Without the split (e7 against e8) it is 12.2 and 15.0, 2.8 us. The transposes of two tiles one behind the other in e7, at 0.50:

```profile
611.92 1.06 PE L731 MATMUL psC<-cpk,wide 128*128 128x128 f32 x4
...
614.48 1.06 PE L731 MATMUL psD<-cpk,wide 128*128 128x128 f32 x4
```

That is 2.56 us for one tile, against 1.30 at 1.00 [rows 3]. What the fall to 0.73 cost in tile 2 no run shows.

**What stays open.** The output stage and what follows take 885.98 to 890.9 us from the first output product to the end, 2.2 less in after than in before, though no instruction there was changed. The kernels with split tiles are at the low end (886.0 to 888.5, e2 at 889.2), e3 and e7 at the high (890.9, 890.6), e8 at 888.6. These are single executions, and the runs of one kernel differ by more (e1 1507.6 to 1516.4), so it may be chance; a cause is not shown. The same holds for the start of the stage.

## What to carry to other kernels

When work is put into an idle engine's list, read what stands behind it there and follow each of its semaphores to the end: one clearing of 0.21 us, 16 us late, cost more than all else in the change. Where two engines are filled to nearly the same degree and exchange each tile over two buffers, do not count with the longer one at 95% of the time: it was busy for 89 and 93% here. And give the new form only a share of the work, where there is much of it per handover: with all tiles split e1 gained nothing; two of three tiles from query tile 3 on, together with the weighing on GpSimd, gained 1%, of which the weighing alone has 0.5%. Last, bring the price of a changed engine from its own kind of operation, or take the upper bound for every question that hangs on when its queue ends.

## What the runs showed of the hardware

GpSimd's multiplication by a column from SBUF costs 2.5 ns a column and 0.3 us (0.61 us for 128 columns, 1.89 for 640, 2.85 for 1024), where VectorE takes 0.55 us for 640 [rows 5] and GpSimd's cast 0.92 ns a column [rows 8]. Beside it VectorE was hardly slowed: the four weighings of 256 columns that stayed there took 349 to 465 ns against 346 to 354 in before, the small factor products of 4 columns their usual 161 to 165, and the worst, one of 8 columns, 616 instead of 168. Two 64-row products into two different banks ran side by side, started 0.01 us apart. A stretch of TensorE's work that took 1.30 us at a granted clock of 1.00 took 2.56 at 0.50.
